# Block 2's mixers: another order of the input product's blocks, the low halves of its weights on VectorE, the convolution's norm and five rotations between the last blocks

## The reference

```
p = hx @ w_in                # 1024 x 1024 by 1024 x 2560: q, k, v (512 each), u (1024)
kc, vc = hc @ w_in[:, 512:1536]        # 256 context tokens: keys and values
q_rot, k_rot = axial_rope(q), axial_rope(k)     # x * cos + swapped(x) * sin
attn = neighbourhood_attention(q_rot, q, k_rot, v, kc, vc, rpb)
h = a * sigmoid(b)           # u = a, b
h = depthwise conv(h), 31 taps, + bias
conv = silu(layer_norm(h) * ln_g + ln_b)
x = x + g1 * (concat(attn, conv) @ w_out)
```

## Time and profile before

| what | value |
|---|---|
| median of 3 runs | 3825.01 us (3813.8, 3825.01, 3825.13) |
| profiled execution, its own time | 3817.68 us |
| its span, first to last instruction | 3816.4 us |
| TensorE, VectorE, ScalarE, GpSimd busy | 87%, 60%, 26%, 11% |
| mean granted TensorE clock | 0.923 |
| blocks of the input product | about 2321 to 2595 us of the span |
| norm, rotations, head of attention | 2595 to 2676 us |

### The profile page before, as it was taken

The page is one execution under the profiler, slowest core; times in us unless marked ns, Lnnn a source line. Parts: engine busy times, 40 slices in busy tenths (PEclk is TensorE's granted clock), DMA queues, the critical chain, the costliest instruction groups (busy, mean ns, idle before and its releaser), DMA issues.

```text
span 3816.4 us, 56694 instructions
## 1 busy us (share of the span) xinstructions
PE 3333.0 (87%) x24667; PEld 2751.8 (72%) x24667; DVE 2303.4 (60%) x3149; ACT 988.7 (26%) x1464; POOL 416.9 (11%) x218
## 2 busy tenths in 40 slices
PE   7988797578887699999999887995888979999997
PEld 5777685367776377888888676783667768888885
DVE  5768475367775444444444565995555656666666
ACT  4543142121110222111111343112445311121122
POOL 2510053000000400000000122220000101111110
PEclk9998798589998699999999998997999989999998
DMA  4400254112111211111111212104000111111111
GB/s 135 131 28 10 67 165 129 35 31 36 29 36 44 94 66 28 50 50 50 50 50 50 77 39 72 45 28 96 1 1 3 54 57 49 45 56 45 46 54 61
DMA packets 261824, 209.29 MB, mean 55 GB/s; under 512 B 87001, under 2 KB 223976, under 8 KB 260936
## 3 DMA queue, kind: packets, MB, share of 16 engines
q1 hardware_dynamic: 247751, 180.50, 16.1%
q10 hardware_dynamic: 13824, 25.17, 2.1%
HBM read 172.84 MB, written 30.95 MB: 53 GB/s over the span
## 4 chain that ended last, share of the span: by engine, by line
PE 70%; DVE 17%; ACT 6%; DMA 2%; POOL 2%; SPq 2%; issue 2%; DVEq 0%; ACTq 0%; POOLq 0%
PE ps L1922 22%; PE ps L1937 15%; PE ps L1785 5%; PE ps L614 4%; PE ps L615 4%; PE ps L616 4%; PE ps L2599 2%; PE ps L1359 2%; PE ps L2577 2%; DVE s_Z L1528 2%; DVE s_tmp L1527 2%; DVE Yc L2506 2%; PE ps L669 1%; PE ps L2587 1%; SPq L1333 1%
## 5 line engine op out<-in xcount | busy, mean ns | idle before, releaser
L2895 DVE TENSOR_TENSOR H<-H,ps 128x1024 f32<-128x1024 f32 x256 | 312.6, 1221 | 182.5 <-PE ps L1937 175.7
L2087 DVE TENSOR_TENSOR fsum<-fsum,ps 128x1024 f32<-128x1024 f32 x168 | 205.1, 1221 | 311.6 <-PE ps L1937 309.4
L1937 PE MATMUL ps<-dh,hh 128*128 128x512 f32 x864 | 340.3, 394 | 17.9 <-DVE hl L1902 13.2
L1937 PE MATMUL ps<-dl,hh 128*128 128x512 f32 x864 | 338.9, 392 | 0.0
L1937 PE MATMUL ps<-dh,hl 128*128 128x512 f32 x864 | 338.9, 392 | 0.0
L1922 PE MATMUL ps<-hn_h,uh 128*128 128x512 f32 x704 | 275.6, 392 | 7.0 <-DVE ul L1626 4.6
L1922 PE MATMUL ps<-hn_l,uh 128*128 128x512 f32 x704 | 274.9, 391 | 0.0
L1922 PE MATMUL ps<-hn_h,ul 128*128 128x512 f32 x704 | 274.8, 390 | 0.0
L1922 PE MATMUL ps<-hx_h,uh 128*128 128x512 f32 x512 | 201.2, 393 | 7.8 <-DVE hx_l L1902 5.3
L1937 PEld LDWEIGHTS ps<-dh,hh 128*128 128x128 f32 x864 | 163.9, 190 | 55.9 <-DVE hl L1902 14.4
L1922 PE MATMUL ps<-hx_l,uh 128*128 128x512 f32 x512 | 201.1, 393 | 0.0
(11 more groups left out here) (473 smaller groups left out, 7734.2 us busy)
## 6 DMA issues: line engine op xcount, KB each, us to landing
aw<-in_w_ada_dram ACTq DMA_DIRECT2D x96, 256.0 KB, 2.9
uw<-in_w_mlp_dram SPq DMA_DIRECT2D x32, 512.0 KB, 4.2
dw<-in_w_mlp_dram SPq DMA_DIRECT2D x32, 512.0 KB, 5.2
uw<-in_ffn_gate_dram SPq DMA_DIRECT2D x22, 512.0 KB, 4.0
uw<-in_ffn_up_dram SPq DMA_DIRECT2D x22, 512.0 KB, 5.3
dw<-in_ffn_down_dram SPq DMA_DIRECT2D x22, 512.0 KB, 6.0
cw<-in_w_in_dram SPq DMA_DIRECT2D x20, 512.0 KB, 3.9
o_w<-in_w_out_dram SPq DMA_DIRECT2D x16, 512.0 KB, 13.5
```

Source lines behind the costliest of these rows:

```text
L1937: mm = pe.e.matmul(ps[:, 2 * pair + hf, :], v[s][:, blk(t)], w[:, half(hf)], start=(m == 0), stop=(m == 2))
L2087: return dve.c.tensor_tensor(f, f, new, ALU.add) if g else dve.c.tensor_copy(f, new)
L2895: return dve.c.tensor_tensor(h, h, self.ps[:, 4 + 2 * (t % 2):6 + 2 * (t % 2), :], ALU.add)
```

## The change

Six things change, all in `mixers2` and at the head of `attention`.

1. Block order: the gates and values of `u` stay first; then the attention's values (8 to 11), keys (12 to 15), queries (16 to 19). The context's product goes with blocks 8 to 15.
2. The low halves of blocks 1 to 19 are made by VectorE, that of block s + 2 right behind block s. The taps are dealt out by block: 0, 2, 7, 7, 7, 7, 7, 7, 9, 12, 12, 12, 12, 10, 8, 5, 0 ...; block 1's gated product goes ahead of the context's preparation.
3. The norm is spread over blocks 15 to 18 and its gain and shift become scale and bias of ScalarE's SiLU.
4. Rotations of keys 0 to 3 and query 1 stand behind blocks 14 to 18, their swaps behind blocks 13 and 15 to 18 (with the norm's three matmul steps, `norm_mean_pe`, `norm_sums_pe` and `norm_over_pe`, behind 16, 17 and 18); queries 0, 3 and 2 remain behind block 19. The product with sin is written back to PSUM; cos and sin lie in the former `glu` and `vT` and are loaded behind block 15's weights.
5. GpSimd clears Qb, Qc and ob once block 19 is done. The mask is added to the bias inside the first four softmax steps.
6. SyncE issues the mask, the small identity and the bias tables behind the norm's sum, `VVo` behind block 19; the end of the stage no longer waits for `VVo`, the first value product does.

```diff
@@ pool_program
-        self.mixers2_pool()
+        self.pool.wait_ge(self.pe["u", 19])
+        for x in (self.Qb, self.Qc, self.ob):
+            self.pool.e.memset(x[:], 0.0).then_inc(*self.pool.one("ob0"))
+        self.meet(self.pool, "mixers2")
@@ in2_blocks
-        return glu + [w[:, PART * n:PART * (n + 1)] for n in range(12)]
+        return glu + [w[:, PART * n:PART * (n + 1)] for n in (8, 9, 10, 11, 4, 5, 6, 7, 0, 1, 2, 3)]
@@ mixers2_sp
         for j in range(2, 20):
-            self.split_load_sp("u", self.cw, blocks, j, self.pool)
+            self.split_load_sp("u", self.cw, blocks, j, self.pool if j == 2 else self.dve)
+            if j == 15:
+                sp.wait_ge(pe["VV", 3])
+                sp.e.dma_start(self.rope[0][:], i["k_rope_cos"]).then_inc(*self.t_misc.one())
+                sp.e.dma_start(self.rope[1][:], i["k_rope_sin"]).then_inc(*self.t_misc.one("rope"))
         sp.wait_ge(dve["ln_sum"])
+        sp.e.dma_start(self.cmask[:], i["k_col_mask"]).then_inc(*self.t_misc.one())
+        sp.e.dma_start(self.aeye[:], i["k_stack_eye"]).then_inc(*self.t_misc.one("a_const"))
...
+        sp.wait_ge(pe["u", 19])
+        sp.e.dma_start(self.VVo[0:64], self.VVe[64:128, 0:NBLK - 1, :]).then_inc(*self.t_in.one())
+        sp.e.dma_start(self.VVo[64:128], self.VVe[0:64, 1:NBLK, :]).then_inc(*self.t_in.one("VV"))
...
-        self.meet(sp, "mixers2", self.t_in["VV"], self.t_st["bias"])
+        self.meet(sp, "mixers2", self.t_st["bias"])
@@ new on TensorE
+    def swap_pe(self, c, src, base, *ready):
+        pe = self.pe
+        pe.wait_ge(self.t_misc["swap"], *ready)
+        for h in range(2):
+            mm = pe.e.matmul(self.ps[:, base + h, :], self.swap[:], src[:, half(h)], start=True, stop=True)
+        mm.then_inc(*pe.one("rope", c))
...
@@ mixers2_pe
+        after = {(j, 0): (lambda j=j: self.context_product_pe(j)) for j in range(8, 16)}
+        for n in range(4):
+            after[9 + n, 1] = lambda n=n: self.values_turn_pe(n)
+        after[13, 1] = lambda: self.swap_pe(4, self.kr[:, 0, :], 6, act["u", 12], act["VV", 3])
+        after[15, 1] = lambda: self.swap_pe(5, self.kr[:, 1, :], 6, act["u", 13], dve["rope", 4])
+        both(16, (self.norm_mean_pe,), (self.swap_pe, 6, self.kr[:, 2, :], 6, act["u", 14], dve["rope", 5]))
+        both(17, (self.norm_sums_pe,), (self.swap_pe, 7, self.kr[:, 3, :], 6, act["u", 15], dve["rope", 6]))
+        both(18, (self.norm_over_pe,), (self.swap_pe, 1, self.q[:, 1, :], 6, act["u", 17], dve["rope", 7]))
+        both(19, (self.swap_pe, 0, self.q[:, 0, :], 4, act["u", 16], dve["conv", 3]),
+             (self.swap_pe, 3, self.q[:, 3, :], 6, act["u", 19], dve["rope", 1]),
+             (self.swap_pe, 2, self.q[:, 2, :], 4, act["u", 18], dve["rope", 0]))
@@ mixers2_act
+                elif j == 16:
+                    self.norm_squares_act()
+                elif j == 17:
+                    self.rsqrt_act("ln", 2 * NBLK)
+                elif j == 18:
+                    self.norm_out_act()
...
+            act.e.activation(self.Yc[:, c, :], self.Yc[:, c, :], ACTF.Silu, scale=self.col("conv_ln_g_2", c), bias=self.col("conv_ln_b_2", c))
@@ mixers2_dve
+        for s in range(20):
+            dve.wait_ge(pe["u", s])
+            if s + 2 < 20:
+                self.split_low_dve("u", self.cw, self.in2_blocks(), s + 2)
+            if s < 8 and s % 2:
...
+            if s == 1:
+                context()
+            for _ in range((0, 2, 7, 7, 7, 7, 7, 7, 9, 12, 12, 12, 12, 10, 8, 5, 0, 0, 0, 0)[s]):
+                next(taps)
+            if s == 14:
+                rope(4, 6)
+            elif s == 15:
+                norm_sum()
+                rope(5, 6)
+            elif s == 16:
+                norm_centre()
+                rope(6, 6)
+            elif s == 17:
+                norm_inverse()
+                rope(7, 6)
+            elif s == 18:
+                norm_scale()
+                rope(1, 6)
+        for c, base in ((0, 4), (3, 6), (2, 4)):
+            rope(c, base)
@@ attention_dve, softmax
+            if t == 0 and u < 4:
+                dve.e.tensor_tensor(self.bias[:, u], self.bias[:, u], rep(self.cmask[:], RPB_R), ALU.add).then_inc(*dve.one("bias"))
+                dve.c
@@ attention_pe, values
+            if t == 0 and u == 0:
+                pe.wait_ge(self.t_in["VV"])
```

More of the change, by code:

```diff
@@ L607, in split_pe @@
             if j not in begun:
-                pe.wait_ge((low or self.dve)[tag, "wl", j])
+                pe.wait_ge((low(j) if low else self.dve)[tag, "wl", j])
                 if j >= 2:
@@ L2383, in values_turn_pe, with norm_mean_pe, norm_sums_pe, norm_over_pe @@
         tr.then_inc(*pe.one("VV", n))
+    def swap_pe(self, c, src, base, *ready):
[4 more added lines that the diff above has]
+        mm.then_inc(*pe.one("rope", c))
+    def norm_mean_pe(self):
+        pe = self.pe
+        pe.wait_ge(self.dve["ln_sum"], self.act["kvc", 15], self.act["VV", 3])
+        for h in range(2):
+            mm = pe.e.matmul(self.ps[:, 4 + h, :], self.ones[:], self.qr[:, 0, half(h)], start=True, stop=True)
+        mm.then_inc(*pe.one("ln_mean"))
+    def norm_sums_pe(self):
+        pe = self.pe
+        pe.wait_ge(self.dve["ln_sq", 3])
+        for t in range(NBLK):
+            mm = pe.e.matmul(self.ps[:, 4, 2 * t:2 * t + 2], self.qr[:, 1, blk(t)], self.ones[:, 0:2], start=True, stop=True)
+        mm.then_inc(*pe.one("ln", "sums"))
+    def norm_over_pe(self):
+        pe = self.pe
+        pe.wait_ge(self.dve["ln", "wide"])
+        for t in range(NBLK):
+            tr = pe.e.transpose(self.ps[:, 4 + t // 4, (t % 4) * PART:(t % 4 + 1) * PART], self.qr[:, 2, blk(t)], self.ident[:])
+        tr.then_inc(*pe.one("ln", "over"))
     def mixers2_pe(self):
@@ L2474, in values_out_act @@
         act.e.activation(self.vc[:, :, blk(n)], self.ps[:, 5, 0:CTX].rearrange("p (a c) -> p a c", a=2), ACTF.Copy).then_inc(*act.one("VV", n))
-    def mixers2_pool(self):
-        pool, blocks = self.pool, self.in2_blocks()
-        for j in range(1, 20):
-            self.split_low(pool, "u", self.cw, blocks, j)
-        self.meet(pool, "mixers2")
     def mixers2_dve(self):
@@ L2508, in conv @@
                     yield
-        taps = conv()
-        for g in range(4):
-            dve.wait_ge(pe["u", 2 * g + 1], act["u", 2 * g])
-            dve.e.tensor_tensor(two(self.cp[:, g, pad:pad + TOK]), two(self.glu[:]), self.bank2(1), ALU.mult).then_inc(*dve.one("u", 2 * g + 1))
-            for _ in range(14 if g < 3 else 4 * TAPS - 42):
-                next(taps)
-        mean, inv, tmp = self.qr[:, 0, :], self.qr[:, 1, :], self.qr[:, 2:4, :]
-        dve.wait_ge(pe["u", 19])
-        dve.c.tensor_tensor(mean, self.Yc[:, 0, :], self.Yc[:, 1, :], ALU.add).then_inc(*dve.one())
@@ L2529, in mixers2_dve @@
-        self.rsqrt_dve("ln", 2 * NBLK, [pe["ln", "sums"]], ALU.mult, 1.0 / RW, ALU.add, 1e-6)
-        self.over_dve("ln", self.st[:, 1, 0:2 * NBLK].rearrange("p (b two) -> p b two", two=2)[:, :, 0:1], tmp[:, 0, :])
-        dve.wait_ge(pe["ln", "over"])
-        for c in range(4):
-            y = self.Yc[:, c, :]
-            dve.c.tensor_tensor(two(y), two(y), ps[:, 6:8, :], ALU.mult).then_inc(*dve.one())
-            dve.c.tensor_scalar(y, y, self.col("conv_ln_g_2", c), self.col("conv_ln_b_2", c), ALU.mult, ALU.add).then_inc(*dve.one("conv", c))
@@ new lines, in norm_inverse, with norm_scale @@
+        def norm_inverse():
+            self.rsqrt_dve("ln", 2 * NBLK, [pe["ln", "sums"]], ALU.mult, 1.0 / RW, ALU.add, 1e-6, src=ps[:, 4, 0:2 * NBLK])
+            self.over_dve("ln", self.st[:, 1, 0:2 * NBLK].rearrange("p (b two) -> p b two", two=2)[:, :, 0:1], tmp[:, 0, :])
+        def norm_scale():
+            dve.wait_ge(pe["ln", "over"])
+            for c in range(4):
+                y = self.Yc[:, c, :]
+                dve.e.tensor_tensor(two(y), two(y), ps[:, 4:6, :], ALU.mult).then_inc(*dve.one("conv", c))
```

128 lines of the change are left out of this document (63 added, 65 removed).

## The result

| | before | after |
|---|---|---|
| median | 3819.41 us (4 runs, 3811.6 to 3825.13) | 3774.66 us (4 runs, 3766.57 to 3777.69) |
| profiled execution, its own time | 3817.68 us | 3766.57 us |
| its span; mean granted clock | 3816.4 us; 0.923 | 3765.3 us; 0.931 |

The ratio is 0.9886 (95%: 0.9859 to 0.9914): 44.7 us faster. The forecast was 3780, from 3764 to 3802.

What follows compares the result with a forecast made beforehand. A string of dependent VectorE steps behind block 2's input-product weight blocks was the bound. Gains of 34.1 + 7.3 - 0.3 = 41 us off 3817.7 give 3776.6; 3.4 on top for the median makes 3780, range 3764 to 3802.

Steps and rivals of the forecast that it cites:

- Low halves and taps: Beside the weight blocks: low halves add 24 us to VectorE, 32 us of tap stretching goes, 8 us net saved.
- Rival B: Taps stay as slow without GpSimd, 1.55 us each, and TensorE waits for low halves from block 12: 3805 us; chance 0.06.
- VectorE's lateness: Beside blocks 9 to 12 VectorE falls back 2 us each time and is 7.9 us late at block 13.
- The new wait: Behind block 15 a swap waits for rotation 4 with block 16 queued behind it: 8.5 us of TensorE idle.
- the dear end: Half clock after the idle behind block 15 costs 5.0 us: 1.9 in the swap, 3.1 in block 16; otherwise 2.6.
- Half clock elsewhere (A): Rival: TensorE pays half clock at every restart of the tail, ending 16 us later: 3796 us; chance 0.15.
- D: Better case: no half clock after block 15, 3775 us; chance 0.76 together with the forecast, the forecast alone 0.6.
- The tail: Behind block 19 one swap of 1.95 us and three rotations of 3.84 each, ending at 2633.2 against 2667.3.
- The head: At attention's head, last rotation to first product falls from 8.5 to 1.2 us, gaining 7.3; softmax additions cost 0.3.
- Transfers: Bias loads end by 2588, hidden; odd values' copies take 8.4 us to land, with 13 us of room.
- Rival C: One serial VectorE queue holds every block; at 1.79 us a tap the profiled time is 3829 us, slower; chance 0.03.
- VectorE idle over 5 us within steps 16 to 18: Sign that the forecast is wrong: such an idle in VectorE's work after blocks 16 to 18.

Runs made afterwards that it cites:

- the run with GpSimd: The changed kernel with the low halves of blocks 2 to 19 made by GpSimd again; median 3780.8 us, ratio 0.9906 to the kernel before.
- the run with the idle filled: The changed kernel with seven unused 128x512 fp32 matmuls added in TensorE's idle behind block 15; median 3768.8 us, ratio 0.9854 to the kernel before.
- the two versions with swaps inside: The changed kernel with swaps of rotation 5, queries 0 and 2 behind blocks' first halves: 3767.3 us; the same with two taps moved earlier: 3766.9 us.

## Why the prediction was right

| step, from block 1's end | forecast | measured (two profiles) |
|---|---|---|
| to the end of block 15 | 184.8 | 183.6, 183.6 |
| blocks 15 to 16, the idle in it | 26.4 | 24.7, 23.9 |
| blocks 16 to 19 | 43.2 | 42.3 |
| block 19 to the last rotation's end | 13.5 | 12.4 |
| last rotation to first product | 1.2 | 1.2 |
| whole stage | 269.1 | 264.3, 263.4 |

**Low halves and taps.** As forecast: 120 taps at 1.285, a low half in each step at 1.22, TensorE without a wait for a low half from block 2 to 15. The sum of 8 us saved on VectorE was right (186.3 against 154.2 + 19 x 1.22 = 177.4), and the run with GpSimd gave 7.1 in the stage. I did not see that this term is worth nothing where VectorE has time to spare. Rival B falls.

**VectorE's lateness.** I had it 7.9 us late at block 13, and it was 8.5 (2523.4 against 2514.8); it runs without idle from 2456.3 to 2568. I had the turn of values at 1.4; the turns took 1.15, and with them the end of block 15 came 1.2 us early.

**The new wait.** Its place, cause and length (8.5, measured 8.87) hold. The swap cost 3.8, as I took it, but the block behind it lost less than the dear end. From block 15 to 16 is 1.7 and 2.5 us shorter than the 26.4 I had, and the run with the idle filled saves only some 2 in the stage.

**Half clock elsewhere (A).** It falls: 1.00 in the blocks from 2561 on, and the mean, sums and turn take 1.88, 1.84 and 1.03. The 11 us of block between the pieces ran at 1.00, as the forecast had it. D's time of 3775 is where the median came to lie, but not for D's reason: there was a half clock; all the steps were a little shorter.

**The tail.** Three rotations at 3.53 instead of 3.84: the product with sin (2616.51) follows on the last addition (2615.37, 1.22 us) without a gap, the swap being done by then. That is 0.9 of the 1.1 us; the swap is the rest (1.73 in place of 1.95).

**The head.** 7.3 forecast, 7.0 by the run that puts it back, and the additions in the softmax cost nothing that can be seen, forecast 0.3. The first of them stands under the first scores (2625.00, 1.16 us, beside products that start at 2624.79). Behind the first product all versions take 1138.6 to 1142.2 us, wherever the additions stand.

**Transfers.** As forecast: the copies of the odd row pairs left at 2611.2 and landed in at most 10.2 us, and the first value product, at 2633.66, waited for nothing.

**What the sum got by luck.** The forecast gain in the stage was 40.4 us (309.5 - 269.1), and 45.2 and 46.0 were measured. The median hides part of this: I put 3.4 us on top of the sum for a median of 3825.0 before, and with a fourth run that median fell to 3819.4. The ends of the range do not follow from their own words either: D at the level of the fastest run gives 3768, not 3764, and A at the level of the median 3800, not 3802. The result lies inside both.

The sum was read from the path and is right as a path, but I never asked what each edit is worth by itself. Had I, I would have priced the order of blocks at nothing. With the deal of taps and the shortened tail, norm and rotations still behind block 19, it gave 20.3 of the 45; how much of that is the order's own is open, by the rows above little. The low halves' move with this deal of taps in the old order makes the kernel slower by 0.24%. Rival C was given its price through dear taps only; its real door is a block that is shorter than the step beside it.

**A sign that was badly set.** "VectorE idle over 5 us within steps 16 to 18" should have shown me wrong. My own times have such a wait (block 18 at 2605.9 against step 17 at 2600.5), and the trace has it, before the four products, and another behind these steps, before rotation 0.

```profile
2598.61 4.62 DVE L2588 TENSOR_TENSOR Yc<-Yc,ps 128x1024 f32<-128x1024 f32 x4 [6.46 <-PE ps L2418]
...
2612.98 1.23 DVE L2557 TENSOR_TENSOR ps<-ps,sin 128x1024 f32<-128x1024 f32 x1 [6.23 <-PE ps L2396]
```

They cost nothing: here TensorE's blocks set the pace.

## What to carry to other kernels

Where two engines that work in strict order feed each other, write a ledger of both, block by block, and compare each step's length with that of the block beside it; the sum of busy time tells little (here the low halves on VectorE were worth a gain of 7.1 us, nothing, or, with a deal of taps made for another order, a loss of 8.8). Price each edit alone as well as in the whole: gains that fill the same free time do not add. When work is interleaved, look for the one instruction that waits in front of a dense block, since it holds up everything queued behind it and leaves the clock to rise again.

## What the runs showed of the hardware

- A GpSimd memset beside VectorE's product with sin, which has one input in PSUM, does not stretch it: 1.23 us, as without company, where a tap beside GpSimd's low half took 3.31. The Trainium skill (SBUF — State Buffer, "Who interferes with whom") says so also of VectorE operations with two SBUF inputs. No run here shows that case: the product with cos starts at 2614.12, behind the end of the last memset at 2613.95, and VectorE stood idle under the first memset. So the price of 0 for the memsets held because almost nothing ran beside them. GpSimd in time, then VectorE, after:

```profile
2612.10 0.95 POOL L568 MEMSET Qc<- 128x1024 f32 x1
2613.00 0.95 POOL L568 MEMSET ob<- 128x1024 f32 x1
...
2612.98 1.23 DVE L2557 TENSOR_TENSOR ps<-ps,sin 128x1024 f32<-128x1024 f32 x1 [6.23 <-PE ps L2396]
2614.12 1.22 DVE L2558 TENSOR_TENSOR qr<-q,cos 128x1024 f32<-128x1024 f32 x1
```

- The stretching is mutual: GpSimd's low half takes 2.62 us on the mean of the 18 in the run with them on GpSimd, nearly all beside taps, and 2.34 alone (2319.14 in the kernel before, with VectorE idle but for its first 0.1 us).
- The same eight bias loads took SyncE 9.08 us to issue from 2565 on; they took 16.2 where they stood before. Nothing was built on it, and no run looked for the reason.
- Behind idles of 3.44 and 4.01 us (in the two versions with swaps inside) the swap took 3.38 and 3.78 us, against 1.88 to 1.98 at full rate. Behind an idle of 2.65 us, in the first of these versions, the mean took 1.98. Behind 2.06 us a swap took 3.32 in one execution of the kernel after and 1.98 in the other.
